# A chain over four chunks with an accumulator per direction, and the bonus and the gate of a group norm computed behind it

## The reference

```python
def wkv_scan(state0, r, decay, kk, b, v, k, reverse):
    def step(S, inp):
        r_t, w_t, kk_t, b_t, v_t, k_t = inp
        sa = jnp.einsum("bhvk,bhk->bhv", S, kk_t)
        S = (S * w_t[:, :, None, :] - sa[..., None] * b_t[:, :, None, :]
             + v_t[..., None] * k_t[:, :, None, :])
        return S, jnp.einsum("bhvk,bhk->bhv", S, r_t)
    ...
    S, ys = lax.scan(step, state0, xs, reverse=reverse)
    return S, jnp.swapaxes(ys, 0, 1)

def rwkv_output(y, r, k, v, g_lo, lp):
    ...
    mu = jnp.mean(y, axis=-1, keepdims=True)
    var = jnp.mean(jnp.square(y - mu), axis=-1, keepdims=True)
    yn = ((y - mu) * lax.rsqrt(var + GN_EPS)).reshape(bsz, t, D_RWKV) * lp["ln_g"] + lp["ln_b"]
    bonus = jnp.sum(to_heads(r) * to_heads(k) * lp["r_k"].astype(jnp.float32), axis=-1, keepdims=True) * to_heads(v)
    gate = jax.nn.sigmoid(g_lo) @ lp["g_up"]
    return ((yn + bonus.reshape(bsz, t, D_RWKV)) * gate).astype(r.dtype)
```

## Time and profile before

| | |
|---|---|
| median of three runs | 1586.79 us (1586.11 to 1588.58) |
| the profiled execution, its own time | 1595.88 us |
| span of its profile, first to last instruction | 1594.1 us |
| busy TensorE / VectorE / ScalarE / GpSimd | 1233.7 / 931.3 / 431.4 / 345.7 us |
| mean granted clock of TensorE | 0.86 |
| line 2057, chain matmuls, both passes | 128 matmuls, 256 records |
| line 2077, chain additions, both passes | 32 |

### The profile page before, as it was taken

How to read it: one execution, slowest core, us unless ns; L and a number is a source line. 1 busy time by engine, 2 the same in 40 slices (tenths; PEclk the granted TensorE clock), 3 DMA queues, 4 the chain that set the end, 5 groups by cost and what they waited for, 6 DMA issues and landing times.

```text
span 1594.1 us, 26618 instructions
## 1 busy us (share of the span) xinstructions
PE 1233.7 (77%) x11250; PEld 842.3 (53%) x11250; DVE 931.3 (58%) x2075; ACT 431.4 (27%) x1087; POOL 345.7 (22%) x315
## 2 busy tenths in 40 slices
PE   7989898893485633457757777799987878999998
PEld 5467784770153200125525443367877854888843
DVE  2887665567897988785677656322345243455512
ACT  3011310132432422553363332323332200111100
POOL 1000011124454544444545444000000000000000
PEclk9997999895587755569958887899999989999999
DMA  9551468699999999999999999433300031544442
GB/s 372 181 194 61 145 213 331 235 334 415 421 417 416 418 422 415 421 406 419 416 419 420 419 415 419 179 110 106 106 9 3 4 107 55 168 145 144 143 152 105
DMA packets 109720, 409.73 MB, mean 257 GB/s; under 512 B 8456, under 2 KB 33552, under 8 KB 76448
## 3 DMA queue, kind: packets, MB, share of 16 engines
q0 software_dynamic: 44576, 297.35, 45.7%
q1 hardware_dynamic: 63552, 106.48, 19.4%
q10 hardware_dynamic: 1472, 4.20, 1.0%
HBM read 405.89 MB, written 2.11 MB: 256 GB/s over the span
## 4 chain that ended last, share of the span: by engine, by line
PE 55%; DMA 21%; DVE 13%; ACT 5%; issue 3%; POOL 2%; another core or an unknown queue 0%; POOLq 0%; DVEq 0%; ACTq 0%
PE psum L502 22%; DMA arena<-in_experts,arena 19%; PE psum L1893 7%; PE psum L512 6%; DVE arena L1438 5%; PE psum L2378 5%; PE psum L1469 3%; POOL arena L1423 2%; DMA weights<-in_w_in 1%; PE psum L748 1%; PE psum L745 1%; PE psum L2262 1%; ACT arena L1449 1%; PE psum L734 1%; PE psum L753 1%
## 5 line engine op out<-in xcount | busy, mean ns | idle before, releaser
L1423 POOL DMA_INDIRECT arena<-in_experts,arena x256 | 315.8, 1233 | 376.4 <-PE psum L1469 297.5
L1469 PE MATMUL psum<-arena 128*32 128x512 f32 x1024 | 193.2, 838 | 248.7 <-ACT arena L1454 248.5
L502 PE MATMUL psum<-actT,weights 128*128 128x256 f32 x1696 | 375.0, 384 | 2.8 <-DVE actT L622 1.0
L502 PEld LDWEIGHTS psum<-actT,weights 128*128 128x128 f32 x1696 | 325.6, 192 | 50.9 <-ACT actT L624 2.6
L1469 PEld LDWEIGHTS psum<-arena 128*32 128x32 f32 x1024 | 23.0, 124 | 349.2 <-ACT arena L1454 338.0
L1438 DVE CUSTOM_DVE_ANT_0 arena<-arena 128x1024 f32<-128x1024 f32 x96 | 116.7, 1224 | 44.8 <-DMA arena<-in_experts,arena 39.6
L1438 DVE CUSTOM_DVE_ANT_0 arena<-weights,arena 128x1024 f32<-128x1024 f32 x96 | 116.5, 1223 | 38.4 <-DMA arena<-in_experts,arena 36.0
L1444 ACT ACTIVATE arena<-arena 128x2 f32<-128x2 f32 x128 | 26.1, 204 | 375.9 <-DVE arena L1438 362.7
L1893 PE MATMUL psum<-arena 64*64 64x64 f32 (+1 forms) x2816 | 87.5, 228 | 18.4 <-DVE arena L2010 7.1
L1893 PEld LDWEIGHTS psum<-arena 64*64 64x64 f32 x2816 | 82.1, 140 | 28.0 <-issue 16.2
L1438 DVE CUSTOM_DVE_ANT_0 arena<-normed,arena 128x1024 f32<-128x1024 f32 x64 | 77.2, 1225 | 20.6 <-DMA arena<-in_experts,arena 19.5
(11 more groups left out here) (392 smaller groups left out, 1716.2 us busy)
## 6 DMA issues: line engine op xcount, KB each, us to landing
weights<-in_w_in SPq DMA_DIRECT2D x18, 2048.0 KB, 8.8
arena<-in_ada_wT POOLq DMA_DIRECT2D x48, 512.0 KB, 5.7
weights<-in_ffn_w_up SPq DMA_DIRECT2D x22, 1024.0 KB, 6.6
weights<-in_ffn_w_down SPq DMA_DIRECT2D x5, 2048.0 KB, 8.0
weights<-in_w_out SPq DMA_DIRECT2D x4, 2048.0 KB, 15.4
weights<-in_w_peer_q SPq DMA_DIRECT2D x4, 2048.0 KB, 11.8
arena<-in_experts,arena POOLq DMA_INDIRECT x256
weights<-in_w_ple_gate SPq DMA_DIRECT2D x2, 2048.0 KB, 7.9
```

The source lines that it names most:

```text
L502: mm = nc.tensor.matmul(out[:, c * T:(c + 1) * T], w[:, k, c * P:(c + 1) * P], act[:, k, :], start=(k == 0), stop=(k == kc - 1))
L1423: nc.gpsimd.indirect_dma_start(out=rows[:, n % RING, :], out_offset=None, in_=dram["experts"], in_offset=bass.IndirectOffsetOnAxis(ap=eidx ...
L1469: mm = nc.tensor.matmul(SUMS[sum_part(k, i), i, :], diag[:, pos, :], rows[:, pos, D + 512 * i:D + 512 * (i + 1)], start=first, stop=last, ...
```

## The change

The two accumulators hold one direction each: `G[d]` takes both partition halves of direction `d`. TensorE waits, multiplies and signals direction by direction, and VectorE adds a direction in one instruction over all 128 partitions. With two additions in a step instead of four, `hist` counts to `2 * step + d`. This holds for the context pass and the token pass.

In the token pass, bonus and gate leave the chain. The four bonus products go into the first solve of the backward direction (`dve_bonus`, woven into `dve_pair` behind its pieces 2 to 5). TensorE forms the bonus means right behind the `y` products, while VectorE adds these to `yT`, and puts them into the last two banks of `AUX`. VectorE multiplies them by `v` and adds `ln_b` when it has added `y`, while TensorE forms the means of `y`. The gate follows the means of `y` on TensorE; it goes to the banks in which the bonus means were, so that it waits for the product with `v`.

```diff
--- before.py
+++ after.py
@@ -2050,11 +2050,10 @@
             for step in range(NCH):
-                pe.wait_ge(S(t + "hist"), 1 + 4 * step)
                 for d in range(2):
+                    pe.wait_ge(S(t + "hist"), 2 * step + d if step else 1)
                     for q in range(RC):
-                        at = (d * RC + q) * HD
                         for g in range(2):
                             part = slice(64 * g, 64 * g + 64)
-                            mm = nc.tensor.matmul(G[g][part, at:at + HD], m.MT[part, d, q, chunk_of(d, step), :],
+                            mm = nc.tensor.matmul(G[d][part, q * HD:(q + 1) * HD], m.MT[part, d, q, chunk_of(d, step), :],
                                                   m.hist[part, step % m.states, d, q, :], start=True, stop=True)
-                            if d == 1 and q == RC - 1:
+                            if q == RC - 1:
                                 mm.then_inc(S(t + "chain"), 1)
@@ -2071,11 +2070,9 @@
             for step in range(NCH):
-                for g in range(2):
-                    part = slice(64 * g, 64 * g + 64)
-                    dve.wait_ge(S(t + "chain"), 2 * step + g + 1)
-                    for d in range(2):
-                        ps = G[g][part, 256 * d:256 * (d + 1)].rearrange("p (q n) -> p q n", q=RC)
-                        nc.vector.tensor_tensor(m.hist[part, (step + 1) % m.states, d], ps, m.N[part, d, :, chunk_of(d, step), :],
-                                                ALU.add).then_inc(S(t + "hist"), 1)
+                for d in range(2):
+                    dve.wait_ge(S(t + "chain"), 2 * (2 * step + d + 1))
+                    ps = G[d][:, 0:RC * HD].rearrange("p (q n) -> p q n", q=RC)
+                    nc.vector.tensor_tensor(m.hist[:, (step + 1) % m.states, d], ps, m.N[:, d, :, chunk_of(d, step), :],
+                                            ALU.add).then_inc(S(t + "hist"), 1)
                 if step == NCH - 1 and not m.full:
-                    dve.wait_ge(S(t + "hist"), 1 + 4 * NCH)
+                    dve.wait_ge(S(t + "hist"), 1 + 2 * NCH)
                     nc.vector.tensor_copy(carry, m.hist[:, NCH % m.states].rearrange("p d q n -> p (d q n)")).then_inc(
@@ -2242,3 +2239,3 @@
             m = x_m
-            pe.wait_ge(S("xhist"), 1 + 4 * NCH)
+            pe.wait_ge(S("xhist"), 1 + 2 * NCH)
             for q in range(RC):
@@ -2254,4 +2251,12 @@
                                 mm.then_inc(S("y_pe"), 1)
-            pe.wait_ge(S("y_dve"), 2)
+            pe.wait_ge(S("y_dve"), RC)
+            head_means([aux[2], aux[3]], x_m.x, "heads_pe")
+            pe.wait_ge(S("y_dve"), RC + 1)
             head_means([aux[0], aux[1]], m.yT, "heads_pe")
+            pe.wait_ge(S("act_load"), act_loaded("gup"))
+            pe.wait_ge(S("y_dve"), RC + 2)
+            for c in range(RC):
+                mm = nc.tensor.matmul(AUX[:, 2 + c // 2, (c % 2) * T:(c % 2 + 1) * T], gup[:, c * P:(c + 1) * P],
+                                      x_m.lora[:, 1, :], start=True, stop=True)
+            mm.then_inc(S("heads_pe"), 1)
 
@@ -2287,13 +2292,3 @@
 
-            steps = pe_chain(pe, x_m, "x")
-            next(steps)
-            pe.wait_ge(S("y_dve"), 1)
-            head_means([aux[0], aux[1]], x_m.x, "heads_pe")
-            next(steps)
-            pe.wait_ge(S("act_load"), act_loaded("gup"))
-            for c in range(RC):
-                mm = nc.tensor.matmul(AUX[:, 2 + c // 2, (c % 2) * T:(c % 2 + 1) * T], gup[:, c * P:(c + 1) * P],
-                                      x_m.lora[:, 1, :], start=True, stop=True)
-            mm.then_inc(S("heads_pe"), 1)
-            all_of(steps)
+            all_of(pe_chain(pe, x_m, "x"))
 
@@ -2301,18 +2296,12 @@
             m = x_m
-
+            all_of(dve_chain(dve, st, m, "x"))
+
+        def dve_bonus(st):
+
+            m = x_m
             for c in range(RC):
-                st.run(nc.vector.scalar_tensor_tensor(m.x[:, c, :], m.r[:, c, :], C("r_k", c), m.k[:, c, :],
-                                                      ALU.mult, ALU.mult))
-            st.settle()
-            dve.sem_inc(S("y_dve"), 1)
-            steps = dve_chain(dve, st, m, "x")
-            next(steps)
-            next(steps)
-            dve.wait_ge(S("heads_pe"), 1)
-            st.link(nc.vector.scalar_tensor_tensor(m.x, AUX[:, 0:2, :].rearrange("p i (c t) -> p (i c) t", t=T),
-                                                   float(HD), m.v, ALU.mult, ALU.mult))
-            next(steps)
-            for c in range(RC):
-                st.run(nc.vector.tensor_scalar(m.x[:, c, :], m.x[:, c, :], C("ln_b", c), None, ALU.add))
-            all_of(steps)
+                ins = nc.vector.scalar_tensor_tensor(m.x[:, c, :], m.r[:, c, :], C("r_k", c), m.k[:, c, :],
+                                                     ALU.mult, ALU.mult)
+                ins.then_inc(S("y_dve"), 1)
+                yield
 
@@ -2330,3 +2319,9 @@
             dve.sem_inc(S("y_dve"), 1)
-            dve.wait_ge(S("heads_pe"), 3)
+            dve.wait_ge(S("heads_pe"), 1)
+            nc.vector.scalar_tensor_tensor(m.x, AUX[:, 2:4, :].rearrange("p i (c t) -> p (i c) t", t=T),
+                                           float(HD), m.v, ALU.mult, ALU.mult).then_inc(S("y_dve"), 1)
+            dve.wait_ge(S("y_dve"), RC + 2)
+            for c in range(RC):
+                st.run(nc.vector.tensor_scalar(m.x[:, c, :], m.x[:, c, :], C("ln_b", c), None, ALU.add))
+            dve.wait_ge(S("heads_pe"), 2)
             st.link(nc.vector.tensor_tensor(m.yT, m.yT, AUX[:, 0:2, :].rearrange("p i (c t) -> p (i c) t", t=T),
@@ -2342,3 +2337,3 @@
             st.settle()
-            dve.wait_ge(S("heads_pe"), 2)
+            dve.wait_ge(S("heads_pe"), 3)
             nc.vector.tensor_tensor(mixed2[:, RC:, :], m.yT, AUX[:, 2:4, :].rearrange("p i (c t) -> p (i c) t", t=T),
@@ -2593,3 +2588,3 @@
             stage(pe=lambda pe, j=j: pe_pair(pe, x_back, "x", 1, j), act=lambda act, j=j: act_pair(act, x_back, "x", 1, j),
-                  dve=lambda dve, st, j=j: dve_pair(dve, st, x_back, "x", 1, j))
+                  dve=lambda dve, st, j=j: woven(dve_pair(dve, st, x_back, "x", 1, j), dve_bonus(st), range(2, 2 + RC) if j == 0 else ()))
         stage(pe=pe_chain_x, dve=dve_chain_x)
```

## The result

The changed kernel takes 1580.07 us (median of 18 runs, 1573.77 to 1589.03), the kernel before, timed beside it, 1587.88 (18 runs, 1584.24 to 1591.87). The ratio is 0.9946 with a 95% interval of 0.9934 to 0.9959: a gain of 8.6 us, between 6.5 and 10.5 (the two medians differ by 7.8). Faster was forecast with 0.93 and is right; the size is not. The forecast gain was 13.0 us, and the median lies 1.1 us above the range that ended at 1579.0. The base is off by as much: the forecast subtracted from 1586.79, the median of three runs, and the 18 runs of before timed beside the changed kernel have 1587.88.

The account below looks back on a forecast made before the run. TensorE and VectorE handing work to and fro alone in the token pass were taken as the bound. -1.73 - 9.46 - 1.90 - 1.85 + 1.93 = -13.0 us, from 1586.79 to 1573.8 us; range 1571.2 to 1579.0, chance 0.70.

Parts of the forecast that it names:

- the term of -1.73: Head of the token chain: with the bonus products moved into a solve's pauses, the carry's copy starts 1.73 us earlier.
- the chain: Token pass, four steps up to the `y` products: 14.50 us before, 5.04 after, with TensorE hardly pausing; -9.46 us.
- The `y` products: TensorE behind the token chain: 6.42 us at first half clock become 4.52 at full clock; -1.90 us.
- the means of `y`: TensorE behind the `y` additions: 3.57 us, at first half clock, become 1.72 with TensorE busy just before; -1.85 us.
- the gate: Gate product on TensorE, moved between the means of `y` and the output product's first six records; adds 1.93 us.
- The stage: Token pass from the last solve's last addition to the output product's sixteen records; 42.7 us before, 29.7 forecast.
- The missing alternation: Rival: in the token chain the second direction waits for the first's addition, eight round trips, 8.7 us; 1577.5 us, chance 0.06.
- the weights as the bound: Rival: the fetch of `rw_out0` and `rw_out1` for the output product sets the pace; no change, about 1586.8 us, chance 0.04.
- the clock low throughout: Last rival: TensorE at half clock from the first chain step until the output product is over; +24.8, 1598.6 us, chance 0.03.
- the first rival: TensorE's clock falls in the token chain and stays low through the `y` products; 5.3 us less gain, 1579.0 us, chance 0.17.
- C: Theory set up after the result: the stretch gains what was forecast, and some 4 us are lost outside it.
- A: Theory set up after the result: the low-clock pieces subtracted are not as long in every old-kernel execution as in the profiled one.

Follow-up runs that it names:

- the fillers: Matmuls with unread products put into TensorE's pauses, in the kernel before (1582.09 and 1582.33 us) and in the changed kernel (1576.37 and 1578.74 us).
- the 82 runs of the table: Timed executions without a trace of kernels with the old token pass (kernel before, or new context chain alone); mean 1587.4 us.
- The changed kernel with fillers: Changed kernel plus unread matmuls ahead of the chain, `y` products, means of `y` and last sixteen records; 1576.37 and 1578.74 us, 0.9932 and 0.9929 against before.
- before with fillers: Kernel before plus unread matmuls ahead of the chain, step 3, `y` products, means of `y` and sixteen records; 1582.09 and 1582.33 us, 0.9968 and 0.9963.

## Why the prediction was right or wrong

**Right, by its own steps.** The carry's copy stands directly behind the last solve's addition, and the bonus products cost nothing in the solve, so the term of -1.73 holds. The addition of 128x256 from PSUM, which no row had shown, takes 424 ns, where 0.42 was taken from the 64x256 form at 418. The directions alternate, and the chain takes 5.44 us from its first matmul to the `y` products, where 5.04 was forecast: a block is 0.73 rather than 0.57, so the round of 1.23 is a little longer than TensorE's 1.15 of work. The `y` products take 4.74 (4.52 forecast), the means of `y` 1.98 (1.72), the gate 1.73 (1.93), the bonus means lie beside the `y` additions, and the variance waits for TensorE. The stage is 30.0 against 29.7.

**The rivals.** The clock did not fall: in seven traces of the new token pass it is 1.00 in the chain and the `y` products. The Trainium skill's "TensorE: Matmul & The Clock Gate", section "A second HAM failure mode: psum-queue depth-cycling", reports that the clock of another kernel, which also cycles through accumulators, swings; no trace here shows it for the new chain. TensorE's timeline of the chain and the start of the `y` products has one piece of 4.89 us, 4.60 of it busy by the window, so seven pauses of about 0.04 us, and 0.55 us behind it:

```profile
1282.56 4.89 PE L2056 MATMUL psum<-arena 64*64 64x64 f32 x128 [1.22 <-DVE arena L2064]
1288.00 0.39 PE L2247 MATMUL psum<-arena 64*64 64x64 f32 x6 [0.55 <-DVE arena L2074]
```

The old chain with bonus and gate moved out has pauses of 1.6 us, and there the clock fell. What each part of the change takes away shows in TensorE's waits in the stage (line that waits, what ended the wait, us in total, times, longest; 2065 and 2064 are the carry, 2330 and 2319 stand behind the `y` additions). Two of before, then the same two of the changed kernel:

```profile
PE psum L2057 <- DVE arena L2065: 3.0, 1, 3.0
PE psum L2281 <- DVEq L2330: 2.6, 1, 2.6
```

```profile
PE psum L2056 <- DVE arena L2064: 1.2, 1, 1.2
PE psum L2286 <- DVEq L2319: 0.7, 1, 0.7
```

The accumulators alone leave the waits of 3.0 and 2.6 us, and the bonus means and the means of `y` behind them stay slow (3.61 and 3.23 us); the move alone leaves those of 1.6 between the steps. This fits that neither half gains by itself. The wait of 2.4 us ahead of the sixteen records is in both kernels, and there the time still varies in the changed one. The waits of before are the same in all its traces, yet its first step takes 1.15 to 1.97 us behind the 3.0: the wait alone does not settle the clock.

The missing alternation, the weights as the bound and the clock low throughout are excluded by the chain of waits and the windows of the changed kernel. The median came close to the first rival's 1579.0, but by chance: nothing of that rival happened. (In the last rival's sum the 13.0 us are passed in the variance already, not in the second six records.)

**The failed step** is the sum's base: "The profiled execution took 1595.88 us, so it would be 1582.9; the median of the runs shown is 9.1 us (0.6%) lower, 1586.79, and the same subtraction gives 1573.8". That takes the 42.7 us of one execution, which lay 9.1 us above the median, to be as long in the median one. Of the 13.0 us, 6.6 hung on a clock of 0.50 in that execution: 0.84 of the first step (1.97 to 1.13), 2.0 of the bonus means (3.71 to 1.72), 1.90 of the `y` products and 1.85 of the means of `y`. The other 6.4 came from the order. With the clock held, the order measured 5.5 us. What is left for the clock is 8.6 - 5.5 = 3.1 us in the times, half of the 6.6. (That the fillers gave the old kernel 5.1 and 5.9 us and the changed one about 2.5, a difference of 3.0, is the same measurement sorted otherwise and no second proof.) Both parts are uncertain by some 3 us either way, so the split is an estimate: the order's part agrees with the forecast, and the clock's part lies below it by little more than the noise. Another 1.1 us of the miss against the range is the base's median of three runs.

The terms were thus right for the traced execution and, as far as the times show, too large for the timed ones. A warning stood in the numbers: 9.1 us between the profiled execution and the median is a gap that has to lie somewhere, and the stretch whose clock had gone up and down was a place for it.

**What stays open.** One unlucky trace explains 42.7 - 41.2 = 1.5 us. The rest is that the old token pass ran longer in all six traced executions than its timed mean. From the times of four kernels and the stages of their traces one can estimate the old stage in the timed executions: 30.0 + 8.3 from the changed kernel, 36.8 + 0 from the accumulators alone, 40.1 - 0.6 from the move alone, 35.9 + 5.5 - 1.7 from the fillers (1.7 of which is in the sixteen records), so about 37 to 40. Of those executions no trace was kept, so this is not shown. The timed executions list a mean granted clock each: within the kernel before, time falls as it rises (the 82 runs of the table, correlation -0.72; 1589.0 us on average at 0.860, 1585.1 at 0.865), and its mean is 0.862, against 0.860 in the traced ones. At 0.8 us per 0.001 that is under 2 of the 4.5 us. Why the traced executions of the old token pass ran longer was not found.

C has no support: the gather takes 670.8 to 672.2 us in the traces, the stretch of the solves 251 to 257, with old and new kernels mixed over the whole of both ranges. A, narrowed to the old stage, is consistent with every run, but for the timed executions it is inferred from the fillers, not seen.

**A version that may be faster still.** The changed kernel with fillers has the lowest ratios in both of its measurements, 0.9932 and 0.9929 against the kernel before, some 2.5 us ahead of the changed one. The intervals of the two overlap, so that lead is not shown.

## What to carry to other kernels

Where an edit removes pauses behind which the clock falls, split the forecast into what the order saves and what the clock saves, and take the second part from several profiled executions, never from one that lies off the median. Fillers in both versions measure that split directly, and may be worth keeping. Two halves of an edit can each be worth nothing while a pause remains somewhere in the stretch: the accumulators alone and the moves alone gained nothing that could be measured here, together 8.6 us.

## What the hardware showed unexpectedly

The `y` products of the changed kernel stop in their middle: the chain of waits has 67 records, an "issue" of 0.53 us, then 61 records. The same pause is in every trace of the new token pass, 0.26 to 0.81 us long. The window around it in the profiled execution, and the `y` products of before with fillers:

```profile
1290.10:1290.80 0.70, 0.17 (x6) 0.08 (x4) 0.00 (x0) 0.00 (x0) 0.00 (x0) 1.00 1.03 386
```

```profile
1298.20:1302.10 3.90, 3.90 (x129) 3.83 (x129) 0.00 (x0) 0.00 (x0) 0.00 (x0) 1.00 0.02 5
```

In the new kernel the products run while the fetch of `rw_out0` and `rw_out1` fills the DMA engines (share 1.03), in the other after it (0.02), and there the same 128 records take 4.00 us without a pause. What the pause waits for was not tested.

The other surprise is that the same program on the same data gives stages of 38.1 to 42.8 us, and sixteen records of 7.13 or 8.83, from one execution to the next: which pauses bring the clock down is not fixed by the program alone.
